# A fast-matmul MLP with fewer weight sums on VectorE: two of four by adding DMAs, and a new order of VectorE's and ScalarE's queues

## What is computed

```
def layer(x):
    x = x + concat([ret_out, conv_out]) @ w_out
    h2 = rms_norm(x, ln2_w)
    x = x + square(relu(h2 @ w_up)) @ w_down      # w_up 1024 x 4096, w_down 4096 x 1024
    return x
```

## Time and profile before

| | |
|---|---|
| runs | 1519.46, 1522.82, 1523.36 us, median 1522.82 |
| profiled execution | 1517.21 us, span 1515.4 us from its first to its last instruction |
| mean granted TensorE clock | 0.979 |
| TensorE matmul busy | 1433.9 us (95%) |
| VectorE, ScalarE, POOL busy | 947.2, 593.2, 131.6 us |
| DMA engines' mean share | 24% |

### The profile page before, as it was taken

The page is one execution under the profiler, slowest core; times in us unless marked ns, Lnnn a source line. Parts: engine busy times, 40 slices in busy tenths (PEclk is TensorE's granted clock), DMA queues, the critical chain, the costliest instruction groups (busy, mean ns, idle before and its releaser), DMA issues.

```text
span 1515.4 us, 22275 instructions
## 1 busy us (share of the span) xinstructions
PE 1433.9 (95%) x8198; PEld 1265.7 (84%) x8198; DVE 947.2 (63%) x1152; ACT 593.2 (39%) x743; POOL 131.6 (9%) x153
## 2 busy tenths in 40 slices
PE   8999999989899899899899999999899999999996
PEld 6888999889689788698688889988887887987985
DVE  6247335396866866867762562535877677677676
ACT  5212222264345345345442113214543543543553
POOL 2433000000000000000043330000000000000001
PEclk9999999999999999999999999999999999999998
DMA  7323111303203303304042221203113213203201
GB/s 254 126 84 113 63 56 57 112 15 112 96 17 112 111 1 112 111 16 153 2 148 97 88 81 63 93 25 121 72 41 111 73 40 111 84 28 112 87 26 70
DMA packets 74677, 124.72 MB, mean 82 GB/s; under 512 B 3332, under 2 KB 20868, under 8 KB 74568
## 3 DMA queue, kind: packets, MB, share of 16 engines
q1 hardware_dynamic: 74424, 123.18, 24.0%
q10 hardware_dynamic: 144, 0.07, 0.0%
HBM read 115.83 MB, written 7.41 MB: 81 GB/s over the span
## 4 chain that ended last, share of the span: by engine, by line
PE 77%; DVE 12%; issue 6%; ACT 4%; POOL 0%; DVEq 0%; DMA 0%; ACTq 0%; POOLq 0%
PE bank L612 22%; PE bank L770 15%; PE bank L622 11%; PE bank L863 11%; PE bank L784 7%; PE bank L876 5%; DVE raws L1798 4%; DVE ring L1775 3%; ACT ring L1132 3%; DVE x L1821 2%; PE bank L662 2%; DVE a_ring L1840 2%; PE bank L700 1%; PE bank L707 1%; PE bank L681 1%
## 5 line engine op out<-in xcount | busy, mean ns | idle before, releaser
L1132 ACT ACTIVATE ring<-raws 128x1024 fp32r<-128x1024 f32 x220 | 231.1, 1055 | 372.6 <-DVE raws L1798 124.3
L1775 DVE TENSOR_TENSOR ring<-raws,ring 128x1024 fp32r<-128x1024 f32 x220 | 268.8, 1222 | 169.2 <-ACT ring L1132 168.3
L863 PE MATMUL bank<-ring,a_ring 128*128 128x512 f32 x1344 | 318.1, 394 | 17.5 <-DVE a_ring L1840 17.5
L770 PE MATMUL bank<-mlp_in_hi,ring 128*128 128x256 f32 x1728 | 320.0, 283 | 0.0
L863 PEld LDWEIGHTS bank<-ring,a_ring 128*128 128x128 f32 x1344 | 254.1, 190 | 74.1 <-issue 20.8
L770 PEld LDWEIGHTS bank<-mlp_in_hi,ring 128*128 128x128 f32 x1728 | 272.1, 191 | 1.4
L770 PE MATMUL bank<-mlp_in_lo,ring 128*128 128x256 f32 x864 | 244.0, 282 | 0.0
L770 PEld LDWEIGHTS bank<-mlp_in_lo,ring 128*128 128x128 f32 x864 | 165.0, 191 | 1.4
L1798 DVE TENSOR_TENSOR raws<-raws 128x1024 f32<-128x1024 f32 x128 | 155.7, 1217 | 0.0
L1359 POOL TENSOR_SCALAR var<-sums 128x1 f32<-128x1 f32 x25 | 9.7, 386 | 1216.4 <-ACT xn L946 1212.8
L622 PE MATMUL bank<-norm_hi,ring 128*128 128x320 f32 x512 | 114.5, 310 | 0.0
(11 more groups left out here) (179 smaller groups left out, 2092.9 us busy)
## 6 DMA issues: line engine op xcount, KB each, us to landing
raws<-in_w_mlp_up SPq DMA_DIRECT2D x32, 1024.0 KB, 7.3
raws<-in_w_mlp_down SPq DMA_DIRECT2D x32, 1024.0 KB, 7.1
w_raw<-in_w_in SPq DMA_DIRECT2D x28, 1024.0 KB, 5.4
w_raw<-in_w_out SPq DMA_DIRECT2D x8, 1024.0 KB, 5.0
past_state<-in_state_ret SPq DMA_DIRECT2D x8, 512.0 KB, 5.1
out_ret_s<-past_state SPq DMA_DIRECT2D x8, 512.0 KB, 4.9
x<-in_x_prompt SPq DMA_DIRECT2D x4, 512.0 KB, 12.5
norm_row<-in_norm_rows SPq DMA_DIRECT2D x3, 512.0 KB, 3.6
```

The lines of the kernel that those rows point to most:

```text
L770: mm = pe.matmul(cols, item_half(item, h, a)[:, k, n * P:(n + 1) * P], mlp_in[i][c][:, k], start=(i in (B11, B21, SUM_1112) and (n, k, m) ...
L863: mm = pe.matmul(out[:], a_item[:, a, 2 * h + k, pair * P:(pair + 1) * P], item_half(item, h, c)[:, k], start=(i in (B11, B21, SUM_1112) a ...
L1132: nc.scalar.activation(item_half(item, h, 0), raw_half(quad, RAW_OF[i], h), ACT.Copy).then_inc(half_hi.sem, 1)
L1775: nc.vector.tensor_tensor(item_half(item, h, 1), raw_half(quad, RAW_OF[i], h), f(item_half(item, h, 0)), ALU.subtract).then_inc(half_lo.se ...
```

## The change

1. `SUMS` holds four sums per quad in place of eight: VectorE makes SUM_1112 and SUM_111222 only. For SUM_1222, a DMA on POOL's queue reads quarter 22 from DRAM and adds it onto quarter 12 in its slot (`accum_op=ALU.add`), after both halves of SUM_1112 are summed. For SUM_ALL, a second one adds quarter 21 onto the slot of 11, after both lo halves of SUM_111222 are made. ScalarE waits for `onto_12` and `onto_11` in place of the sums. These are 32 transfers of 1 MB in all.
2. `SLOTS`: quarter 11 of the next quad goes where 21 was, since 21 is free after product 1; the four loads of the next quad wait for the lo halves of products 1, 4, 5, 6, in the order 11, 12, 21, 22.
3. In an up quad, the sample part of product 5 (B22) comes before its halves.
4. The lists of ScalarE and VectorE are put in another order; the sum SUM_1112 of a quad is made at the end of the quad before.
5. `tail` shares its place with `sample_hidden`, and `dynamic_dma_scratch_size` goes from 1024 to 2048.

```
-SLOTS = [(0, 1, 2, 3), (2, 3, 1, 0), (1, 0, 3, 2), (3, 2, 0, 1)]
+SLOTS = [(0, 1, 3, 2), (3, 1, 2, 0), (2, 1, 0, 3)]
-SUMS = [(SUM_1112, 0), (SUM_1112, 1), (SUM_111222, 0), (SUM_111222, 1), (SUM_1222, 0), (SUM_1222, 1), (SUM_ALL, 0),
-        (SUM_ALL, 1)]
+SUMS = [(SUM_1112, 0), (SUM_1112, 1), (SUM_111222, 0), (SUM_111222, 1)]
...
+                    for i, name in ((B21, "11"), (SUM_1222, "12"), (B22, "21"), (SUM_ALL, "22")):
+                        sp.wait_ge(half_lo.sem, half_lo.at(layer, 2 * (first + i) + 2))
+                        settle(sp)
+                        load_quarter(layer, quad, name)
...
+                        if i == B22 and b == 0:
+                            pe.wait_ge(in_diff_lo.sem, in_diff_lo.at(layer, 4))
+                        if i in (SUM_1222, B22):
                             up_sample(b, i)
...
+                    elif i == SUM_1222:
+                        act.wait_ge(onto_12.sem, onto_12.at(layer, 16 * (quad + 1)))
+                    elif i == SUM_ALL:
+                        act.wait_ge(onto_11.sem, onto_11.at(layer, 16 * (quad + 1)))
```

The transfers on POOL's queue:

```
+                def add_onto(quad, onto, name, done):
+                    src = (for_up, for_down)[quad % 2]
+                    settle(pool)
+                    pool.dma_start(raws[:, slot_of(quad, onto)],
+                                   src[bass.ds(layer, 1), quad // 2, int(name[0]) - 1, int(name[1]) - 1
+                                       ].rearrange("l p k c -> (l p) k c"), accum_op=ALU.add).then_inc(done.sem, 16)
+                for quad in range(QUADS):
+                    pool.wait_ge(weights_summed.sem, weights_summed.at(layer, sums_to(quad, SUM_1112, 1)))
+                    add_onto(quad, "12", "22", onto_12)
+                    pool.wait_ge(half_lo.sem, half_lo.at(layer, 2 * (quad * PRODUCTS + SUM_111222) + 2))
+                    add_onto(quad, "11", "21", onto_11)
```

ScalarE's list (indent cut):

```
         copy_product(b, B11, 0)
-        weight_half(item + 2, 0)
         copy_product(b, B11, 1)
         if b == 0:
             for c in range(2):
                 read_turn(layer, ("n2", NT - 1, c))
             in_diff_hi_of(0)
+        weight_half(item + 2, 0)
         weight_half(item + 2, 1)
-        weight_half(item + 3, 0)
         if b == 0:
             in_diff_hi_of(1)
             in_diff_hi_of(2)
+        square_hidden(b, h11, B21, 1.0)
+        weight_half(item + 3, 0)
+        weight_half(item + 3, 1)
         sample_square(b, 0)
-        weight_half(item + 3, 1)
-        square_hidden(b, h11, B21, 1.0)
         weight_half(item + 4, 0)
         if b == 0:
             in_diff_hi_of(3)
             in_diff_hi_of(4)
+        weight_half(item + 4, 1)
         read_back(b, 0)
-        weight_half(item + 4, 1)
-        copy_product(b, SUM_111222, 0)
         a_item_hi(b, B11)
         weight_half(item + 5, 0)
+        copy_product(b, SUM_111222, 0)
         copy_product(b, SUM_111222, 1)
         weight_half(item + 5, 1)
         copy_product(b, SUM_1222, 0)
...
         copy_product(b, SUM_1222, 1)
         weight_half(item + 6, 1)
         square_hidden(b, h22, SUM_1222, -1.0)
+        sample_square(b, 1)
         weight_half(item + 7, 0)
-        sample_square(b, 1)
+        weight_half(item + 7, 1)
         square_hidden(b, h12, B22, -1.0)
-        weight_half(item + 7, 1)
-        read_back(b, 1)
         a_item_hi(b, B21)
         weight_half(item + 8, 0)
+        read_back(b, 1)
 
     def down(b):
         item = (2 * b + 1) * PRODUCTS
         last_quarter(b)
         weight_half(item + 1, 1)
         mid_diff_hi(b)
+        a_item_hi(b, SUM_1112)
         weight_half(item + 2, 0)
-        a_item_hi(b, SUM_1112)
         weight_half(item + 2, 1)
+        a_item_hi(b, SUM_111222)
         weight_half(item + 3, 0)
-        a_item_hi(b, SUM_111222)
         weight_half(item + 3, 1)
         weight_half(item + 4, 0)
+        weight_half(item + 4, 1)
         a_item_hi(b, SUM_1222)
-        weight_half(item + 4, 1)
         weight_half(item + 5, 0)
+        weight_half(item + 5, 1)
         a_item_hi(b, B22)
-        weight_half(item + 5, 1)
         weight_half(item + 6, 0)
+        weight_half(item + 6, 1)
         a_item_hi(b, SUM_ALL)
```

VectorE's list:

```
-        weight_sum(q, SUM_1112, 0)
+            weight_sum(q, SUM_1112, 0)
         weight_half(item + 1, 1)
         if b == 0:
+            weight_sum(q, SUM_1112, 1)
             read_turn_lo(layer, ("n2", NT - 2, 1))
-        weight_sum(q, SUM_1112, 1)
-        weight_half(item + 2, 0)
-        if b == 0:
             read_turn_lo(layer, ("n2", NT - 1, 1))
             in_diff_lo_of(0)
+            in_difference(0)
+            in_difference(1)
+        weight_half(item + 2, 0)
         weight_half(item + 2, 1)
         weight_sum(q, SUM_111222, 0)
         if b == 0:
-            in_difference(0)
-            in_difference(1)
-        hidden_sum(b, B21, 0)
-        weight_half(item + 3, 0)
-        hidden_sum(b, B21, 1)
-        weight_sum(q, SUM_111222, 1)
-        if b == 0:
             in_diff_lo_of(1)
             in_difference(2)
-        weight_half(item + 3, 1)
-        weight_sum(q, SUM_1222, 0)
+        hidden_sum(b, B21, 0)
+        weight_sum(q, SUM_111222, 1)
+        hidden_sum(b, B21, 1)
         if b == 0:
             in_diff_lo_of(2)
+        weight_half(item + 3, 0)
+        weight_half(item + 3, 1)
         weight_half(item + 4, 0)
-        weight_sum(q, SUM_1222, 1)
         if b == 0:
             in_diff_lo_of(3)
             in_diff_lo_of(4)
+        weight_half(item + 4, 1)
         sample_lo(b, 0)
-        weight_half(item + 4, 1)
-        weight_sum(q, SUM_ALL, 0)
+        a_item_lo(b, B11)
         weight_half(item + 5, 0)
-        a_item_lo(b, B11)
-        weight_sum(q, SUM_ALL, 1)
         weight_half(item + 5, 1)
         hidden_sum(b, SUM_1222, 0)
         weight_half(item + 6, 0)
         hidden_sum(b, SUM_1222, 1)
         weight_half(item + 6, 1)
         hidden_sum(b, B22, 0)
+        weight_half(item + 7, 0)
+        weight_sum(q + 1, SUM_1112, 0)
         hidden_sum(b, B22, 1)
-        weight_half(item + 7, 0)
         weight_half(item + 7, 1)
-        sample_lo(b, 1)
+        weight_sum(q + 1, SUM_1112, 1)
         a_item_lo(b, B21)
         weight_half(item + 8, 0)
+        sample_lo(b, 1)
 
     def down(b):
         q, item = 2 * b + 1, (2 * b + 1) * PRODUCTS
-        weight_sum(q, SUM_1112, 0)
+        a_difference(b, SUM_1112)
         weight_half(item + 1, 1)
-        a_difference(b, SUM_1112)
-        sample_lo(b, 2)
-        weight_half(item + 2, 0)
         a_difference(b, SUM_1222)
         for p in range(2):
             add_to_x(b, B11, p)
-        weight_sum(q, SUM_1112, 1)
         a_item_lo(b, SUM_1112)
+        a_difference(b, SUM_111222)
+        weight_half(item + 2, 0)
+        weight_half(item + 2, 1)
         weight_sum(q, SUM_111222, 0)
-        weight_half(item + 2, 1)
-        a_difference(b, SUM_111222)
+        weight_sum(q, SUM_111222, 1)
+        sample_lo(b, 2)
+        a_item_lo(b, SUM_111222)
+        a_difference(b, B22)
         weight_half(item + 3, 0)
+        weight_half(item + 3, 1)
+        add_to_x(b, B21, "sample")
+        weight_half(item + 4, 0)
         for p in range(2):
             add_to_x(b, B21, p)
-        add_to_x(b, B21, "sample")
-        weight_sum(q, SUM_111222, 1)
-        a_item_lo(b, SUM_111222)
-        weight_half(item + 3, 1)
-        weight_sum(q, SUM_1222, 0)
-        a_difference(b, B22)
-        weight_half(item + 4, 0)
+        weight_half(item + 4, 1)
+        a_item_lo(b, SUM_1222)
         for p in range(2):
             add_to_x(b, SUM_1112, p)
-        weight_sum(q, SUM_1222, 1)
-        a_item_lo(b, SUM_1222)
-        weight_half(item + 4, 1)
-        weight_sum(q, SUM_ALL, 0)
         weight_half(item + 5, 0)
         for p in range(2):
             add_to_x(b, SUM_111222, p)
-        weight_sum(q, SUM_ALL, 1)
+        weight_half(item + 5, 1)
         a_item_lo(b, B22)
-        weight_half(item + 5, 1)
         weight_half(item + 6, 0)
         for p in range(2):
             add_to_x(b, SUM_1222, p)
+        weight_half(item + 6, 1)
+        a_item_lo(b, SUM_ALL)
         add_to_x(b, B22, "sample")
-        a_item_lo(b, SUM_ALL)
-        weight_half(item + 6, 1)
         if b < NBLK - 1:
             weight_half(item + 7, 0)
+            weight_sum(q + 1, SUM_1112, 0)
         for p in range(2):
             add_to_x(b, B22, p)
         if b < NBLK - 1:
             weight_half(item + 7, 1)
+            weight_sum(q + 1, SUM_1112, 1)
```

More of the change, by code:

```diff
@@ L144, in mlp_steps @@
             out.append(("up", b, i, 1))
-            if i in (B11, B21, B22):
+            if i in (B11, B21):
                 out.append(("up sample", b, i))
@@ L166, in half_used @@
     if quad % 2 == 0:
-        return STEP["up sample", b, i] if i in (B11, B21, B22) else STEP["up", b, i, h]
+        return STEP["up sample", b, i] if i in (B11, B21) else STEP["up", b, i, h]
```

(10 more changed lines are left out.)

78 lines of the change are left out of this document (28 added, 50 removed).

## The result

| | before | after |
|---|---|---|
| median of the runs | 1521.14 us (4 runs, 1517.62 to 1523.36) | 1440.68 us (4 runs, 1439.91 to 1441.11) |
| profiled execution, its span | 1517.21, 1515.4 us | 1440.67, 1439.0 us |

The ratio is 0.9473, with a 95% interval of 0.9451 to 0.9494: 5.3% faster, 80.5 us by the medians and 76.4 us by the two spans. The forecast was 1446 us, and 1440 for the profiled execution; that one took 1440.67.

A forecast was written before the change was run, and what follows sets the result against it. TensorE, busy 1433.9 of 1515.4 us, was taken as the bound, losing time to waits for VectorE and half clock. Removing 77 us took the profiled 1517.2 to 1440; plus 5.6 gave 1446 us, range 1434 to 1488.

The forecast's parts named there:

- The bound and the quads: TensorE's MLP quads without waits for VectorE: 51.9 us up and 49.0 us down.
- The sum of 77 us: Whole kernel: down quads gain 63.2 us, up quads but the first 17.7, first quads lose 3.8.
- The first up quads: Each layer's first up quad: TensorE waits 5.9 us ahead of the sample's transpose, not later; costs 1.9 us per layer.
- Why VectorE was late: Down quads: a relay of sum, hi, lo takes 7 us for two halves, against 5.44 us of TensorE per product.
- The sample's part of product 5: Up quads: moved to the front, it frees half 0 of item 5 at 42.9 instead of 45.7, without TensorE cost.
- The adding DMA: Each 1 MB transfer on POOL's queue takes 11 us, between bounds of 5.4 and 21.9, and is hidden.
- The cover of it: Time to hide the adding DMAs: 19 us for the second transfer, some 21 us for the first before ScalarE notices.
- point of no gain: Adding DMAs: the 77 us are used up when a transfer takes 22 us, with 1.6 us of half clock counted.
- rival 2: The adding DMA is late and ScalarE's hi halves wait: slower, 1648 us at 30 us per transfer; chance 0.11.
- The spare times: Steady quads: operands are ready 1.6 to 4 us before they are wanted.
- rival 1: Leftover waits of 2 us in each down quad, 1469 us, or in all 16 quads, 1492; chance 0.18.
- The median: The median of runs lies 5.6 us above the profiled execution's 1440, so 1446 us is forecast.

The follow-up runs named there:

- e_dma: Changed kernel with the old order of ScalarE's and VectorE's lists (less the DMAs' sums) and product 5's sample part behind its halves: 1460.93 us, ratio 0.961.
- e_order_s5: Changed kernel's list order, all eight sums on VectorE, no adding DMAs, old slots and loads, product 5's sample part behind its halves: 1474.74 us, ratio 0.9692.
- e_order: Changed kernel's list order and early sample part, but all eight sums on VectorE, no adding DMAs, slots and loads of before: 1445.35 us, ratio 0.9506.
- e_first: Changed kernel with own lists for each layer's first up quad: sample's square and items 3 and 4 ahead of h11's square, hidden sums, late differences: 1427.18 us.
- e_samp5: Changed kernel with the sample's part of product 5 behind its halves again in up quads: 1453.38 us, ratio 0.956.
- e_copy: Changed kernel with plain copies in place of the adding transfers (accum_op left out, two sums then wrong): 1443.64 us, one run.
- e_late6: Changed kernel with 6 chained small POOL operations ahead of each adding DMA, to delay it: 1501.93 us, ratio 0.9874.
- e_late10: Changed kernel with 10 chained small POOL operations ahead of each adding DMA, to delay it: 1540.61 us, ratio 1.0128.
- e_s5: Kernel before with one thing changed, the sample's part of product 5 of an up quad ahead of its halves: 1516.63 us, ratio 0.9953.

## Why the prediction was right, point by point

Medians of all runs of the three parts, in us (a dash: not run). "DMAs" takes in the change's slots and order of loads:

| | sample part behind | sample part first | and own first-quad lists |
|---|---|---|---|
| old lists, eight sums | 1521.1 | 1516.6 | – |
| old lists, DMAs | 1460.9 | – | – |
| new lists, eight sums | 1474.7 | 1445.4 | 1439.4 |
| new lists, DMAs | 1453.4 | 1440.7 | 1427.2 |

And the quads by TensorE's timeline in the profiled executions, in us from first matmul to first matmul:

| | first up quad of layer 0, 1 | other up quads | down quads |
|---|---|---|---|
| before | 59.6, 60.3 | 54.0 in layer 0, 55.6 in layer 1 | 56.8 to 57.1 |
| `e_dma` | 55.7, 55.7 | 52.0 | 52.9 to 53.2 |
| `e_order_s5` | 62.4, 62.2 | 52.0 | 53.2 to 53.3 |
| `e_order` | 62.2, 61.9 | 52.0 | 49.3 to 49.4 |
| the change | 62.1, 61.7 | 52.0 | 49.1 |
| `e_first` | 54.4, 54.4 | 52.0 | 49.1 |

So either the DMAs or the new lists clear the steady up quads, and the down quads come to 49 us only with the new lists and the sample's part first (the old lists with the DMAs and the sample's part first were not run). The new lists as the change has them cost 6 us in each first up quad: `e_samp5`, with the new lists and all else as in `e_dma`, takes 61.9 and 62.1 us there against 55.7.

**The bound and the quads.** Right. The quads without waits, added up from rows of before, were 51.9 and 49.0 us; all quads but the first of a layer are now 52.0 and 49.1. The sum of 77 us stands against 76.4 in the two spans. By layers too: 31.6 + 6.3 − 1.9 = 36.0 us in the first, where the second MLP now begins at 1015.8 in place of about 1050.6, 35 us earlier; 41.1 in the second, where 76.4 − 35 = 41 are measured.

**The first up quads.** Right in place, size and cause: 5.9 us ahead of the transpose were predicted, 5.73 came, twice, and `e_first` takes them away. The price of 1.9 us for each such quad came out at 2.5 and 1.4. The prediction put the wait down to the new order, rightly; it did not ask whether the first quad needs that order, and `e_dma` with the old lists takes 55.7 us there.

**Why VectorE was late.** The relay in the earlier trace rows is real, and the second half of the prediction's sentence on the sums held: what counts is not the 77.9 us of VectorE's work but that products 4 and 6 need no sum from it. `e_dma` takes the sums out from between the halves of products 4 and 5 in the old lists, and product 4's wait all but goes while product 3's stays. But the prediction gave one price for all parts together, and the parts stand in for each other. The DMAs in the old lists bring 60 us. The new order with the sample's part first brings 76 without one sum taken away. The two together bring 80.5, not 136. That each of them breaks the same relay is the reading that fits the waits of these runs. The sum of the prediction holds for the change as a whole, which has all parts in it; it would have been wrong for the DMAs alone or the sample's part alone, and would have come out for the new order with the sample's part first, where no sum is taken away.

**The sample's part of product 5.** Priced at nothing ("at no cost to TensorE"). Undone in the changed kernel it costs 12.7 us and with eight sums 29.4; done alone it brings 4.5 to 6 us by the medians, which the spread of the runs can explain. The prediction's own times held the reason: the square of the sample stands in ScalarE's queue ahead of item 7. It looked at what the earlier part frees, and not at what its old place would hold up in the new list.

**The adding DMA.** Predicted 11 us, measured 8.4 to 10.2 with medians of 9.5 and 8.8, inside the bounds of 5.4 and 21.9. The Trainium skill (Collectives: The Full Stack, "The bandwidth ceiling: the fold count and why AG ≠ RS ≠ AR") has a reducing transfer of a ring collective go at half the rate of a copy, as it reads two sources. The adding DMA here is a local one, so the page bears on it by analogy. `e_copy` agrees in direction and not in size: the landing takes 1.6 times that of the plain transfer at the same place, what is fixed in both included. For the sum it made no difference.

**The cover of it.** 18.6 to 18.9 us in up quads for the predicted 19, but 16 to 18 in down quads; and a wait has some 2.0 us of half clock behind it (1.7 in the mean of `e_late6`) and not 1.6. The prediction's point of no gain, 22 us, is therefore too far: at 19.3 us in up and 21.7 in down quads (`e_late6`, third block) 61 of the 80 us were gone, at 21.9 and 22.7 (`e_late10`) the kernel was 1.3% slower than before. In the changed kernel the slowest transfer lands 10.2 us after its issue, 11 after its condition, 5 us or more ahead of the shortest cover, so rival 2 didn't come. The other reason given for rival 2, the Trainium skill's page SBUF — State Buffer, the box "The 'DVE blocks DMA' trap (SWDGE)", was not put to the test: VectorE's work in the MLP is of two operands, as the prediction says, and none of it of the kind that the page names. Beside this work, with VectorE 61% busy, the 32 issues take 1.283 to 1.489 us and none stands out.

**The spare times** of 1.6 to 4 us held in every quad; rival 1 didn't come. `e_samp5` shows how thin they are: 2 to 4 us later at one place of ScalarE's queue leave 0.9 us of wait in each down quad.

**The median.** The 5.6 us added to the profiled execution's 1440 were the distance of before's median from its profiled execution. The runs of before spread over 1513 to 1524 us, those after over 1439.9 to 1441.1. The whole miss of 5.3 us is this term, and the traces show most of where it comes from. In the profiled execution of before the same wait of 1.77 or 1.78 us in the up quads is followed by the full clock in layer 0 and by a lower one in layer 1 (windows right behind it; the clock is the third number from the end):

```profile
562.90:566.40 3.50, 3.41 (x17) 2.92 (x18) 3.48 (x5) 2.59 (x4) 0.00 (x0) 1.00 0.00 0
1198.70:1202.20 3.50, 3.45 (x10) 2.69 (x11) 3.48 (x4) 2.55 (x4) 0.00 (x0) 0.60 0.00 0
```

That is 54.0 against 55.6 us for such a quad. In the trace of `e_s5`, 1523.3 us with the same wait there, the six quads all take 55.6 or 55.7 us, and the three of layer 0 alone are 4.9 of the 6.1 us between the two executions. The changed kernel has no such waits, and so nothing for which the term could have stood: the prediction carried a spread of before over to a kernel from which it had removed the cause.

## What to carry to other kernels

Before an engine is relieved of work, try the order of its queue: here the order and one moved TensorE step brought 76 of 80 us with the same work, and the relief brought 60 in the old order. Look at the first round of the loop by itself, too: the list that was right for the steady quads cost 6 us in each first one. Price two levers on one wait each alone and both together; their sum is no forecast. A transfer that is to be hidden has its cover at each place in the loop, and the shortest of them, with the other transfers that fall in it, decides.

## What the runs showed of the hardware

A DMA of 1 MB that adds onto SBUF on POOL's queue lands in 8.4 to 10.2 us in the changed kernel (up to 11.8 in `e_samp5`), a plain one there in 5.2 to 7.8, and POOL is held 1.29 and 0.75 us by the issue. In a quad of `e_late6` where a load of another queue went out during its issue, an adding one took 12.6 us (the longest of that run 12.7). A chain of dependent operations on POOL of 128x4 elements costs 1.25 us each, about twice what I had set in for it. Behind one and the same wait of 1.78 us ahead of an up quad's sample part the granted clock of the next 3.5 us was 1.00 in three quads of before and 0.60 to 0.61 in three others. The loads of `raws` on SP's queue landed in 5.7 us for up quads, where they took 7.3. The waits are not what did it: with the old slots and order of loads the median is 9.0 us in `e_order`, whose steady quads have no waits, and with the new ones 5.6 in `e_dma`, which has them. Which part of the new way of loading does it was not tried.
